# A two-layer encoder trunk in three-term fp32: last head pair filled further, operand orders at the feed-forward, unread retention states

## The chip, the cores and the metric

The kernel runs on one core of a Trainium2 chip. The metric is the device time of one execution in microseconds. A core has five engines that run their own instruction streams and meet at semaphores: TensorE (PE, matmuls into PSUM), VectorE (DVE), ScalarE (ACT), GpSimd (POOL) and SyncE (SP), which here issues all DMAs.

## What is computed

The reference, cut to its two layers. Layer 0 mixes tokens by bidirectional retention (six heads of 128), layer 1 by two-dimensional neighbourhood attention (twelve heads of 64, taken in six pairs); beside either stand four memory heads, and a SwiGLU feed-forward follows each. There are 1024 tokens of width 1024, a hidden width of 2816 and 256 memory tokens.

```
a = rms_norm(h, norm_g[i, 0])
y = retention_layer(a, ...) if i % 2 == 0 else na_layer(a, ...)     # concat heads and memory heads, @ w_out
h = h + rms_norm(y, norm_g[i, 1])
a = rms_norm(h, norm_g[i, 2])
gate, up = jnp.split(a @ ffn_w_in[i], 2, axis=-1)
h = h + rms_norm((jax.nn.silu(gate) * up) @ ffn_w_out[i], norm_g[i, 3])

# retention, one direction, chunks of 128 tokens
kv = jnp.einsum('bhncd,bhnce->nbhde', kc * k_dec, vc)
def step(state, kv_n):
    return state * chunk_dec + kv_n, state
_, prev = lax.scan(step, jnp.zeros((b, h, dk, dv)), kv)
out = out + jnp.einsum('bhncd,nbhde->bhnce', qc * q_dec, prev)
```

## The kernel before

**Products.** A large product is made of three matmuls (`three`, L2111 to L2116): each operand is split into a rounded part ("hi", written by ScalarE) and a remainder ("lo", written by VectorE for activations and by GpSimd for weights), and hi·hi, hi·lo and lo·hi are summed in PSUM. Weights come in units of 128 x 1024 through a ring of three slots: SP loads `stage` (`load_units`), ScalarE writes `whi` (`his`, L1057), GpSimd writes `wlo` (`los`, L827), and TensorE's last use frees the slot. All orders are written out by hand: each engine's program lists its operations, and a step waits for semaphore counts.

**Turnings.** `turn` number t transposes normed token tiles into `aT` or `AOP`: TensorE transposes, ScalarE evicts piece k as hi (L1104), VectorE makes lo (L1561). In `first_two` (turnings 2 and 6, ahead of each layer's mixer) the second half of the tokens is turned in two parts of four pieces (`turn_late`, L2158) among the first products.

**Retention.** Per head `chunk_states` multiplies keys by values for eight chunks and both directions (L2504), VectorE's `scan` runs the recurrence, and `chunk_outputs` adds three products per chunk (L2515 to L2517). The forward state of chunk 0 and the backward state of chunk 7 are zero.

**Feed-forward.** Its input and output products are a two-level scheme with seven products in place of eight. `AOP` holds seven operands: 1 and 2 are halves of the turned tokens, the others are sums ("7", "6", "5", "3") and the second tokens' late pieces ("4"), made on VectorE by `turn_second` (L1642 to L1659) and `lo_second` (L1666). Weight operands come from ScalarE (`operand_hi`, L1143) and GpSimd (`combine` L904, `operand_lo` L880). `hidden_sum` (L1681) adds a product's bank to what is there; product "4" waits for the sums "6" and "7". `turn_second` of TensorE (L2254, L2262) makes the late pieces; its last one waits for `gate_out(l, 5)` (L1163).

**Passage.** After the output product of a feed-forward, VectorE scales (L1589), adds the residual (`post_add`, L1598) and norms (`post_scale`, L1549), four token tiles each; ScalarE squares; GpSimd makes the factors (`post_factor` L854 to L856, `pre_factor` L839 and L840). In layer 0 the split of the unit U_NA + 1 stands behind all four squares on ScalarE and behind all four `post_factor` on GpSimd.

**Attention.** Six head pairs of 16 tiles; step T of 96 (+4) has scores, peak, exponential, scaling, transposes and values of neighbouring tiles on different engines. `filler(T)` puts one projection piece of the next pair (two matmul triples) into each step. For the last pair t = T - 80 counts its tiles; there 24 output rows (each one triple, first set, pieces k = 0 to 5) are spread over t = 1 to 19:

```
                if 0 < t < LAST:
                    for m in range(24 * (t - 1) // (LAST - 1), 24 * t // (LAST - 1)):
                        out_rows(1, 0, m // TT, range(m % TT, m % TT + 1), first_set_free(1))
```

The pieces of the concatenated heads are stored to HBM (`store_cat`) and fetched back (`cat_back`, L582) over the space of `aT` once all projections are made, then split by `cat_split` (ScalarE L1365, VectorE L1887) at t = 0, 2, 5, 8, 11, 14; pieces 6 and 7 follow behind the pair (`out_phase`), and piece 7 is written in place. `take_k` (L2065) copies a pair's keys, `take_q` its queries.

## Time and profile before

| | us |
|---|---|
| median of 3 runs | 2304.22 (2302.72 to 2304.95) |
| the profiled execution, its own time | 2304.31 |
| its span | 2302.5 |
| TensorE / weight load busy | 2245.8 (98%) / 1840.5 (80%) |
| VectorE / ScalarE / GpSimd busy | 1227.9 (53%) / 902.1 (39%) / 1074.2 (47%) |
| DMA | 279.11 MB, mean 121 GB/s |

The span runs from the first to the last instruction in the trace; the execution's own time has 1.8 us more. Busy time of TensorE is that of its matmuls; weight loads run beside them. An engine's idle time is put down to what released the instruction behind it; idle time of an engine that nobody waits for costs nothing. In the chain of work that ended last, TensorE has 87% of the span. A row of a timeline gives start and duration in us, then in brackets the idle time before it and what ended that. A row of a stretch (A:B) gives its length, the busy us and number of instructions of PE, PEld, DVE, ACT and POOL, TensorE's granted clock as a share of full speed, the busy share of the DMA engines, and GB/s.

### The profile page before, as it was taken

What the parts mean: (1) busy time and instruction counts of PE and PEld (TensorE: products, weight loads), DVE (VectorE), ACT (ScalarE), POOL (GpSimd) and SP (SyncE); (2) the same over time, 40 slices, a digit from 0 to 9 for tenths busy, and PEclk for the clock granted to TensorE, in tenths of its full rate; (3) what the DMA queues carried; (4) which work ended last, traced back from release to release, by engine and by line L of the source; (5) the groups of instructions that cost most, each with busy time, mean ns of one, the idle gap of its engine ahead of it and who ended that gap; (6) DMA issues with size and microseconds to landing.
All of it is one profiled execution on the core that took longest, in us unless ns stands there. A gap on an engine that the chain in (4) does not pass through costs nothing.

```text
span 2302.5 us, 32169 instructions
## 1 busy us (share of the span) xinstructions
PE 2245.8 (98%) x11948; PEld 1840.5 (80%) x11948; DVE 1227.9 (53%) x2065; ACT 902.1 (39%) x1793; POOL 1074.2 (47%) x777
## 2 busy tenths in 40 slices
PE   7999999999999999999999999999999999999998
PEld 6788888888788888888879867767878888888886
DVE  4644444546654444577753255555575444347767
ACT  5531111256223333344654345554642333334443
...
GB/s 215 46 83 46 47 46 46 129 167 108 115 132 138 110 96 110 214 213 95 107 178 102 138 91 103 68 129 120 193 81 131 159 103 108 103 103 327 97 96 156
DMA packets 138573, 279.11 MB, mean 121 GB/s; under 512 B 34531, under 2 KB 55602, under 8 KB 136370
## 3 DMA queue, kind: packets, MB, share of 16 engines
...
q14 instruction: 59, 0.48, 0.1%
HBM read 207.80 MB, written 69.23 MB: 120 GB/s over the span
## 4 chain that ended last, share of the span: by engine, by line
PE 87%; DVE 3%; POOL 2%; ACT 1%; issue 1%; DMA 1%; SPq 0%; DVEq 0%; POOLq 0%; ACTq 0%
PE PS L2114 26%; PE PS L2116 26%; PE PS L2115 26%; PE PS L2396 2%; PE PS L2583 2%; PE PS L2601 2%; PE PS L2504 1%; POOL wlo L827 1%; DVE SB L1851 1%; PE PS L2429 1%; PE PS L2492 1%; PE PS L2384 1%; POOL rstd L856 0%; PE PS L2517 0%; PE PS L2516 0%
## 5 line engine op out<-in xcount | busy, mean ns | idle before, releaser
L2114 PE MATMUL PS<-AOP,OPS 128*128 128x512 f32 x1216 | 474.3, 390 | 5.1 <-DVE AOP L1666 3.2
L2116 PE MATMUL PS<-AOP,OPS 128*128 128x512 f32 x1216 | 473.5, 389 | 0.0
L2115 PE MATMUL PS<-AOP,OPS 128*128 128x512 f32 x1216 | 473.4, 389 | 0.0
L827 POOL TENSOR_TENSOR wlo<-stage,whi 128x1024 fp32r<-128x1024 f32 (+1 forms) x88 | 207.8, 2366 | 407.5 <-ACT whi L1057 407.2
L880 POOL TENSOR_TENSOR OPS<-TW,OPS 128x512 fp32r<-128x512 f32 x176 | 260.8, 1497 | 77.3 <-ACT OPS L1143 77.3
L2114 PE MATMUL PS<-aT,whi 128*128 128x512 f32 (+1 forms) x672 | 273.7, 407 | 7.3 <-DVE bdK L1917 3.6
L2114 PEld LDWEIGHTS PS<-AOP,OPS 128*128 128x128 f32 x1216 | 228.3, 188 | 54.4 <-POOL OPS L880 4.0
L2116 PEld LDWEIGHTS PS<-AOP,OPS 128*128 128x128 f32 x1216 | 228.3, 188 | 47.5
L2115 PEld LDWEIGHTS PS<-AOP,OPS 128*128 128x128 f32 x1216 | 228.4, 188 | 47.1
L2116 PE MATMUL PS<-aT,wlo 128*128 128x512 f32 (+1 forms) x672 | 261.4, 389 | 0.0
L2115 PE MATMUL PS<-aT,whi 128*128 128x512 f32 (+1 forms) x672 | 260.5, 388 | 0.0
L2114 PE MATMUL PS<-OPS 128*128 128x512 f32 x616 | 240.3, 390 | 1.8 <-DVE Y L1756 1.8
L2116 PE MATMUL PS<-OPS 128*128 128x512 f32 x616 | 239.9, 389 | 0.0
L2115 PE MATMUL PS<-OPS 128*128 128x512 f32 x616 | 239.8, 389 | 0.0
L1143 ACT ACTIVATE OPS<-TW 128x512 fp32r<-128x512 f32 x176 | 106.5, 628 | 338.1 <-POOL TW L904 315.9
L880 POOL TENSOR_TENSOR OPS<-stage,OPS 128x512 fp32r<-128x512 f32 x128 | 173.4, 1358 | 53.1 <-ACT OPS L1143 48.8
L839 POOL TENSOR_SCALAR msq<-sumsq 128x1 f32<-128x1 f32 x42 | 23.5, 560 | 361.2 <-ACT junk L1076 359.5
L1681 DVE TENSOR_TENSOR up<-PS,u 128x512 f32<-128x512 f32 x88 | 60.8, 691 | 226.5 <-PE PS L2116 224.9
L1270 ACT ACTIVATE OPS<-SRAW 128x512 fp32r<-128x512 f32 x154 | 97.4, 632 | 206.8 <-PE PS L2116 206.8
L1713 DVE TENSOR_TENSOR OPS<-SRAW,OPS 128x512 fp32r<-128x512 f32 x154 | 106.3, 690 | 96.7 <-ACT OPS L1270 96.5
L2114 PEld LDWEIGHTS PS<-aT,whi 128*128 128x128 f32 x672 | 128.4, 191 | 34.8 <-issue 11.9
L2116 PEld LDWEIGHTS PS<-aT,wlo 128*128 128x128 f32 x672 | 128.0, 191 | 26.5
...
## 6 DMA issues: line engine op xcount, KB each, us to landing
stage<-in_w SPq DMA_DIRECT2D x100, 512.0 KB, 3.8
hidden_scratch<-HT SPq DMA_DIRECT2D x154, 256.0 KB, 2.2
SRAW<-hidden_scratch SPq DMA_DIRECT2D x154, 256.0 KB, 2.6
...
```

Source lines behind the costliest of these rows:

```text
L827: pool.tensor_tensor(wlo[:, slot, cols], stage[:, slot, cols], whi[:, slot, cols].bitcast(F32), ALU.subtract)\
L880: pool.tensor_tensor(place[:, 1, :], w1_operand(l, j, p), place[:, 0, :].bitcast(F32), ALU.subtract)\
L1143: act.activation(op_place(q)[:, 0, :], w1_operand(l, j, p), ACT.Copy).then_inc(o_hi, 1)
L1270: act.activation(OPS[:, s_op, 0, :], SRAW[:, s_slot(q), :], ACT.Copy).then_inc(g_hi, 1)
L1681: dve.tensor_tensor(dst, PS[:, in_bank(l, j, p), :], with_, ALU.add).then_inc(f_ed, 1)
L1713: dve.tensor_tensor(OPS[:, slot, 1, :], src, OPS[:, slot, 0, :].bitcast(F32), ALU.subtract).then_inc(g_lo, 1)
L2114: pe.matmul(dst, stat[0], mov[0], start=start, stop=False, skip_group_check=onto)
L2115: pe.matmul(dst, stat[0], mov[1], start=False, stop=False, skip_group_check=onto)
L2116: return pe.matmul(dst, stat[1], mov[0], start=False, stop=stop, skip_group_check=onto)
L2396: ins = pe.transpose(PS[0:keys, banks(r)[1], c * P:(c + 1) * P], SB[:, r % 3, c * width:c * width + keys], ident[:, :])
L2583: ins = pe.matmul(dst, qpair[half, g % 2, t, :], keys[:, :, (GW - KC) * w:(GW - KC) * w + KC], start=True, stop=True)
L2601: ins = pe.matmul(PS[half, 7, (t % 4) * GW:(t % 4 + 1) * GW], Vc[0:keys, g % 2, place, half], PT[0:keys, r % 3, col:col + GW], start=(c == ...
```

## The change

- Retention: the state products of chunk 0 (backward half) and chunk 7 (forward half), and the two output products with zero states, are left out.
- Turnings 2 and 6: the first part of `turn_late` now turns six pieces, the second two; the second waits for two remainders instead of four, and a new wait for six stands ahead of the second halves of the first unit.
- Feed-forward entry: VectorE splits piece 7 ahead of the first `post_add`; ScalarE does `gate_out(l, 5)` ahead of `raw_second`; VectorE does `lo_second` ahead of the sums "6" and "7".
- Passage in layer 0: the split of U_NA + 1 moves behind the second tile on ScalarE and GpSimd, and VectorE's scales lag two tiles behind its sums. An exponential of one column is issued ahead of the memory queries' copies.
- Attention: queries are copied in two halves, one step apart, with the weight split behind. In the last pair 28 output rows are spread over t = -1 to 18, pieces are split at t = -3, -1, 1, 3, 6, 9, 13, the first three are fetched while the last key unit is still projected (a new semaphore `k_last` counts its pieces), units U_OUT1 + 3, + 4, + 5 are split at t = 6, 12, 17 (before, + 3 at 11 and the others in `out_phase`), and three units more are loaded ahead of the next phase.

The diff, with renumbered waits left out and one line of context:

```diff
@@ -239,6 +239,7 @@
             sem(n) for n in ("s_mm", "s_add", "s_exp", "s_nrm", "s_tr", "pt_ev", "pv", "o_ev"))
+        k_last = sem("k_last")
         v_mm, v_ea, v_ed = sem("v_mm"), sem("v_ea"), sem("v_ed")
@@ -284,7 +285,11 @@
                 return 4 - D0[t // 4] + k % 4
-            return 4 + k % 4 if t in (2, 6) else k % 4 if t == 5 else k
+            if t in (2, 6):
+                return (4, 5, 6, 7, 1, 3, 4, 5)[k]
+            return k % 4 if t == 5 else k
+        LATE = 6
@@ -363,6 +368,8 @@
             return [item for at, item in enumerate(FIRST) if sum(cost[:at]) * steps // sum(cost) == t]
+        SPLIT_AT = (-3, -1, 1, 3, 6, 9, 13)
@@ -573,10 +580,10 @@
-            def cat_back(l, th, tiles):
+            def cat_back(l, th, tiles, free=None):
                 cols = slice(HALF * th, HALF * th + HALF)
-                sp.wait_ge(*USED[U_OUT[l] - 1])
+                sp.wait_ge(*(free or USED[U_OUT[l] - 1]))
                 for k in tiles:
@@ -793,18 +800,21 @@
             for hp in range(1, HP):
+                if hp == HP - 1:
+                    for k in range(3):
+                        cat_back(1, 0, [k], (k_last, 2 * k + 2))
                 load_units(U_NAH + 2 * hp + 7)
...
                 if hp == HP - 1:
-                    cat_back(1, 0, range(KD - 2))
+                    cat_back(1, 0, range(3, KD - 2))
                 store_cat(9 + hp)
...
             load_units(U_OUT1 + 5)
-            cat_back(1, 1, range(KD - 2))
-            for th in range(2):
-                cat_back(1, th, [KD - 2])
+            cat_back(1, 0, [KD - 2])
+            cat_back(1, 1, range(KD - 1))
+            load_units(U_OUT1 + 8)
             before_out(1)
@@ -959,19 +969,20 @@
                     post_factor(1 + 2 * l, 1, i)
+                    if l == 0 and i == 1:
+                        los(U_NA + 2)
                 if l == 0:
-                    los(U_NA + 2)
                     for i in range(TT):
...
-            pool.memset(minus_half[:, :], -0.5).then_inc(mh_rdy, 1)
-            pool.wait_ge(mh_rdy, 1)
+            pool.memset(minus_half[:, :], -0.5).then_inc(zer, 1)
+            pool.wait_ge(zer, 1)
             pre(0)
...
             pool.memset(kprod[:, :, :], 0.0).then_inc(zer, 1)
-            pool.wait_ge(zer, 2)
+            pool.wait_ge(zer, 3)
             los(2)
@@ -1092,7 +1103,7 @@
                         act.wait_ge(t_low, t // 4 + 1)
-                    if t in (2, 6) and k == 4:
+                    if t in (2, 6) and k == LATE:
                         act.wait_ge(t_done, turned(t))
@@ -1190,9 +1201,6 @@
                 U, s, t = U_OUT[l], 2 * l, 4 * l + 3
-                if l:
-                    his(U + 5)
-                    cat_split(l, range(KD - 2, KD - 1))
                 cat_split(l, range(KD - 1, KD))
@@ -1237,8 +1245,8 @@
                 operand_hi(l, 8)
+                gate_out(l, 5)
                 raw_second(l)
-                gate_out(l, 5)
                 hi_second(l)
@@ -1305,8 +1313,8 @@
                     square(Y1[:, i, 0:HALF], total(N_T + 8 * s + TT + i), g_ed, 24 * l + 21 + i, y_sq)
-                if l == 0:
-                    his(U_NA + 2)
+                    if l == 0 and i == 1:
+                        his(U_NA + 2)
                 post_out(s, 1)
@@ -1476,15 +1484,16 @@
             act.wait_ge(h_new, 16)
+            act.activation(gvar[:, 0:1], minus_half[:, 0:1], ACT.Exp)
             take(U_NA, MQ[:, 0, :])
...
-            def take_q(n, dst):
+            def take_q(n, dst, halves=range(2)):
                 act.wait_ge(*USED[n])
                 act.wait_ge(g_used, N_OUT_FF)
-                for th in range(2):
+                for th in halves:
                     for w in range(2):
@@ -1492,7 +1501,8 @@
                             ACT.Copy, scale=0.125)
-                ins.then_inc(ev_act, 1)
+                if 1 in halves:
+                    ins.then_inc(ev_act, 1)
@@ -1519,17 +1529,14 @@
                 t = T - (HP - 1) * ROWS
-                if t < 0 and T % KD == KD - 2:
-                    n = next_unit(T)
-                    if T % ROWS < KD:
-                        take_q(n, qpair[:, (T // ROWS + 1) % 2, :, :])
-                    his(n + RING + 1)
-                if t == 0:
-                    cat_split(1, range(1))
-                if t in (2, 5, 8, 11, 14):
-                    cat_split(1, [(t + 1) // 3])
-                    if t == 11:
-                        his(U_OUT1 + 4)
+                if t < 0 and T % ROWS in (KD - 2, KD - 1):
+                    take_q(next_unit(T), qpair[:, (T // ROWS + 1) % 2, :, :], (T % ROWS - KD + 2,))
+                if t < 0 and T % ROWS in (KD - 1, ROWS - 2):
+                    his(next_unit(T) + RING + 1)
+                if t in SPLIT_AT:
+                    cat_split(1, [SPLIT_AT.index(t)])
+                if t in (6, 12, 17):
+                    his(U_OUT1 + 4 + (6, 12, 17).index(t))
             out_phase(1)
@@ -1625,9 +1632,8 @@
                 post_half(s, 1, 1, 0)
-                turn(t, range(6, 7))
+                turn(t, range(6, 8))
                 post_add(s, 1, 0)
-                turn(t, range(7, 8))
                 for i in range(1, TT):
@@ -1766,9 +1772,9 @@
                 turn_second(l)
+                lo_second(l)
                 hidden_sum(l, 0, "6")
                 hidden_sum(l, 0, "7")
-                lo_second(l)
                 hidden_sum(l, 0, "5")
@@ -1813,7 +1819,11 @@
                         post_in_late(s, i - 1, 0)
-                post_out(s, 1)
+                for i in range(TT + 2):
+                    if i < TT:
+                        post_add(s, 1, i)
+                    if l == 0 and i >= 2:
+                        post_scale(s, 1, i - 2)
@@ -2100,10 +2110,8 @@
                     take_k(next_unit(T))
-                if t == 0:
-                    cat_split(1, range(1))
-                if t in (2, 5, 8, 11, 14):
-                    cat_split(1, [(t + 1) // 3])
+                if t in SPLIT_AT:
+                    cat_split(1, [SPLIT_AT.index(t)])
             out_phase(1)
@@ -2147,15 +2155,15 @@
                 if part:
-                    pe.wait_ge(a_lo, a_before(t) + 4)
+                    pe.wait_ge(a_lo, a_before(t) + KD - LATE)
                 elif t == 6:
...
                         pe.wait_ge(xs, tiles_before(t) + i + 1)
-                    for k in range(4):
-                        f = (4 * part + k) * P
-                        ins = pe.transpose(PS[:, 4 + k, i * P:(i + 1) * P], set_tiles(t)[:, i, f:f + P], ident[:, :])
+                    for k in range(LATE, KD) if part else range(LATE):
+                        ins = pe.transpose(PS[:, turn_bank(t, k), i * P:(i + 1) * P],
+                                           set_tiles(t)[:, i, k * P:(k + 1) * P], ident[:, :])
                     if part:
@@ -2178,6 +2186,8 @@
                     ins.then_inc(w_used, 1)
+                elif n == U_OUT1 - 1:
+                    ins.then_inc(k_last, 1)
@@ -2210,6 +2220,8 @@
                 turn_late(t, 1)
+                pe.wait_ge(a_lo, a_before(t) + LATE)
                 for k in range(KD):
@@ -2355,8 +2367,8 @@
                 t = 4 * l + 3
-                for k in range(6, KD):
-                    out_rows(l, 0, k, range(2 if l == 0 and k == 6 else 0, TT))
+                for k in range(6 + l, KD):
+                    out_rows(l, 0, k, range(2 if k == 6 else 0, TT))
                 for st, free in ((1, second), (2, third)):
@@ -2500,9 +2512,10 @@
                         pe.wait_ge(st_rdy, h)
-                    bank = (2, 3, 0, 1)[c // 2]
-                    ins = pe.matmul(PS[:, bank, 256 * (c % 2):256 * (c % 2) + 256], Ktok[:, c, :],
-                                    vfb[:, c, :, :].rearrange("p a c -> p (a c)"), start=True, stop=True)
+                    bank, at_c = (2, 3, 0, 1)[c // 2], 256 * (c % 2)
+                    d0, d1 = (0, 1) if c == 0 else (1, 2) if c == 7 else (0, 2)
+                    ins = pe.matmul(PS[:, bank, at_c + P * d0:at_c + P * d1], Ktok[:, c, :],
+                                    vfb[:, c, d0:d1, :].rearrange("p a c -> p (a c)"), start=True, stop=True)
                 ins.then_inc(kv_mm, 1)
@@ -2513,8 +2526,10 @@
                     pe.matmul(dst, ST[:, c, :], V[:, c, :], start=True, stop=False)
-                    pe.matmul(dst, qfb[:, 0, cc], states[:, c, 0, :], start=False, stop=False)
-                    ins = pe.matmul(dst, qfb[:, 1, cc], states[:, c, 1, :], start=False, stop=True)
+                    if c > 0:
+                        ins = pe.matmul(dst, qfb[:, 0, cc], states[:, c, 0, :], start=False, stop=(c == 7))
+                    if c < 7:
+                        ins = pe.matmul(dst, qfb[:, 1, cc], states[:, c, 1, :], start=False, stop=True)
                 ins.then_inc(out_mm, 1)
@@ -2608,8 +2623,8 @@
                     project(U_NAH + 2 + piece // KD, piece % KD)
-                if 0 < t < LAST:
-                    for m in range(24 * (t - 1) // (LAST - 1), 24 * t // (LAST - 1)):
+                if 0 <= t + 1 < LAST:
+                    for m in range(28 * (t + 1) // LAST, 28 * (t + 2) // LAST):
                         out_rows(1, 0, m // TT, range(m % TT, m % TT + 1), first_set_free(1))
...
             tiles = HP * ROWS
```

How it moves instructions, at three places. VectorE at the first feed-forward entry, from the last remainder of a sum on (L1659, now L1665); L1666 (now L1672) is `lo_second`, L1681 (now L1687) the sums. Before:

```order
L1659 TENSOR_TENSOR AOP<-S1R,AOP 128x2048
L1681 TENSOR_TENSOR u_96<-PS,s_95 128x512
L1681 TENSOR_TENSOR up_97<-PS,u_96 128x512
L1666 SCALAR_TENSOR_TENSOR AOP<-PS,gT,AOP 128x512 x4
L1681 TENSOR_TENSOR up_97<-PS,up_97 128x512
L1659 TENSOR_TENSOR AOP<-RAWA,AOP 128x2048
L1681 TENSOR_TENSOR sg_99<-PS,u_96 128x512
L1681 TENSOR_TENSOR up_100<-PS,u_96 128x512
```

and with the change:

```order
L1665 TENSOR_TENSOR AOP<-S1R,AOP 128x2048
L1672 SCALAR_TENSOR_TENSOR AOP<-PS,gT,AOP 128x512 x4
L1687 TENSOR_TENSOR u_96<-PS,s_95 128x512
L1687 TENSOR_TENSOR up_97<-PS,u_96 128x512
L1687 TENSOR_TENSOR up_97<-PS,up_97 128x512
L1665 TENSOR_TENSOR AOP<-RAWA,AOP 128x2048
L1687 TENSOR_TENSOR sg_99<-PS,u_96 128x512
L1687 TENSOR_TENSOR up_100<-PS,u_96 128x512
```

The four remainders of the late pieces moved ahead of two sums.

VectorE in the passage behind layer 0's feed-forward: L1589 (now L1596) scales by the gains, L1598 (now L1605) is `post_add`, L1549 (now L1556) `post_scale`, L1561 (now L1568) the turning. Before:

```order
L1589 TENSOR_TENSOR Y_104<-Y_104,gB 128x512 x2
L1598 SCALAR_TENSOR_TENSOR Hb<-Y_104,rstd,Hb 128x1024 x2
L1549 TENSOR_SCALAR Y_104<-Hb,rstd 128x1024
L1598 SCALAR_TENSOR_TENSOR Hb<-Y_104,rstd,Hb 128x1024
L1549 TENSOR_SCALAR Y_104<-Hb,rstd 128x1024
L1598 SCALAR_TENSOR_TENSOR Hb<-Y_104,rstd,Hb 128x1024
L1549 TENSOR_SCALAR Y_104<-Hb,rstd 128x1024 x2
L1561 SCALAR_TENSOR_TENSOR aT<-PS,gT,aT 128x512 x8
```

and with the change:

```order
L1596 TENSOR_TENSOR Y_104<-Y_104,gB 128x512 x2
L1605 SCALAR_TENSOR_TENSOR Hb<-Y_104,rstd,Hb 128x1024 x3
L1556 TENSOR_SCALAR Y_104<-Hb,rstd 128x1024
L1605 SCALAR_TENSOR_TENSOR Hb<-Y_104,rstd,Hb 128x1024
L1556 TENSOR_SCALAR Y_104<-Hb,rstd 128x1024 x3
L1568 SCALAR_TENSOR_TENSOR aT<-PS,gT,aT 128x512 x8
```

Three sums now stand ahead of the first scale.

TensorE from the scores of the tiles before the last pair on (t = -2 and -1): L2583 (now L2598) scores, L2601 (now L2616) values, L2396 (now L2408) transposes, `whi,catT` an output row. Before:

```order
L2583 MATMUL PS<-kTn,qpair 64x320 x4
L2601 MATMUL PS<-PT,Vc 64x64 x12
L2396 MATMUL PS<-ident,SB 120x128 x2
L2396 MATMUL PS<-ident,SB 80x128
L2396 MATMUL PS<-ident,SB 120x128 x2
L2396 MATMUL PS<-ident,SB 80x128
L2583 MATMUL PS<-kTn,qpair 64x320 x4
L2601 MATMUL PS<-PT,Vc 64x64 x12
L2396 MATMUL PS<-ident,SB 120x128 x2
L2396 MATMUL PS<-ident,SB 80x128
L2114 MATMUL PS<-whi,catT 128x512
L2115 MATMUL PS<-wlo,catT 128x512
```

and with the change:

```order
L2598 MATMUL PS<-kTn,qpair 64x320 x4
L2616 MATMUL PS<-PT,Vc 64x64 x12
L2408 MATMUL PS<-ident,SB 120x128 x2
L2408 MATMUL PS<-ident,SB 80x128
L2122 MATMUL PS<-whi,catT 128x512
L2123 MATMUL PS<-wlo,catT 128x512
L2124 MATMUL PS<-whi,catT 128x512
L2408 MATMUL PS<-ident,SB 120x128 x2
L2408 MATMUL PS<-ident,SB 80x128
L2122 MATMUL PS<-whi,catT 128x512
L2123 MATMUL PS<-wlo,catT 128x512
L2124 MATMUL PS<-whi,catT 128x512
```

An output row stands behind each tile's transposes, where none stood before.

## Rows read from the trace of the kernel before

**Rows 1.** The page, part 1: busy us, share of the span and instructions of each engine

```profile
PE 2245.8 (98%) x11948; PEld 1840.5 (80%) x11948; DVE 1227.9 (53%) x2065; ACT 902.1 (39%) x1793; POOL 1074.2 (47%) x777
```

**Rows 2.** Waits of TensorE: engine, line, releaser: us in total, times, longest us

```profile
PE PS L2114 <- DVE AOP L1666: 3.2, 2, 1.6
...
PE PS L2158 <- DVE Y L1549: 3.5, 3, 2.0
...
PE PS L2114 <- DVE AOP L1561: 1.5, 2, 0.8
...
PE PS L2262 <- ACT Hb L1163: 2.7, 2, 1.4
...
PE PS L2396 <- DVE SB L1851: 2.7, 6, 0.7
...
PE PS L2114 <- POOL wlo L827: 2.5, 2, 1.4
...
PE PS L2114 <- issue: 2.3, 1, 2.3
...
PE PS L2114 <- DVE catT L1887: 1.6, 1, 1.6
```

**Rows 3.** Timeline of TensorE, first head: start us, us, engine, line, operation, tiles, xcount

```profile
152.01 2.05 PE L2492 MATMUL PS<-qT,kT 128*128 128x128 f32 x16 [0.30 <-ACT Ktok L1440]
...
164.82 3.61 PE L2504 MATMUL PS<-vfb,Ktok 128*128 128x256 f32 x16
```

**Rows 4.** Timeline of TensorE and VectorE around the first layer's second turning

```profile
47.06 1.91 PE L2158 MATMUL PS<-ident,Y 128*128 128x128 f32 x16
...
49.73 2.73 DVE L1561 SCALAR_TENSOR_TENSOR aT<-PS,gT,aT 128x512 fp32r<-128x512 f32 x4 [7.13 <-ACT aT L1104]
...
54.23 0.48 PE L2114 MATMUL PS<-aT,whi 128*128 128x512 f32 x1
```

**Rows 5.** Timeline of ScalarE, VectorE and GpSimd, first feed-forward entry

```profile
551.36 2.42 ACT L1173 ACTIVATE RAWB<-PS,gT 128x512 f32<-128x512 f32 x4 [2.56 <-PE PS L2254]
...
570.90 3.38 DVE L1659 TENSOR_TENSOR AOP<-S1R,AOP 128x2048 fp32r<-128x2048 f32 x1
...
578.22 2.72 DVE L1666 SCALAR_TENSOR_TENSOR AOP<-PS,gT,AOP 128x512 fp32r<-128x512 f32 x4
...
581.60 3.35 POOL L904 TENSOR_TENSOR TW<-stage,TW 128x512 f32<-128x512 f32 x1
...
585.12 1.30 POOL L904 TENSOR_TENSOR TW<-stage,TW 128x512 f32<-128x512 f32 x1 [0.17 <-POOL TW L904]
```

**Rows 6.** Timeline of the passage, and the stretch from 1190 to 1194 us

```profile
1176.30 2.47 DVE L1598 SCALAR_TENSOR_TENSOR Hb<-Y,rstd,Hb 128x1024 f32<-128x1024 f32 x2
...
1177.96 3.04 POOL L827 TENSOR_TENSOR wlo<-stage,whi 128x1024 fp32r<-128x1024 f32 x1
...
1185.00 1.28 DVE L1598 SCALAR_TENSOR_TENSOR Hb<-Y,rstd,Hb 128x1024 f32<-128x1024 f32 x1
...
1188.46 0.75 DVE L1549 TENSOR_SCALAR Y<-Hb,rstd 128x1024 f32<-128x1024 f32 x1 [0.71 <-POOL rstd L840]
...
1189.28 1.10 PE L2158 MATMUL PS<-ident,Y 128*128 128x128 f32 x4 [0.81 <-DVE Y L1549]
...
1190.00:1194.00 4.00, 4.00 (x14) 3.20 (x13) 2.73 (x4) 2.42 (x4) 0.00 (x0) 0.66 0.00 0
```

**Rows 7.** The last head pair: its stretch, timeline of VectorE and GpSimd, one DMA issue

```profile
1528.40:1592.00 63.60, 54.55 (x491) 37.34 (x490) 34.73 (x96) 33.29 (x88) 10.62 (x5) 1.00 0.39 133
...
1528.33 1.28 DVE L2065 COPY kTn<-PS 128x512 f32<-128x512 f32 x2
...
1530.52 2.33 DVE L1851 TENSOR_SCALAR SB<-SB,rowinv 128x320 f32<-128x320 f32 x1
...
1530.31 2.36 POOL L827 TENSOR_TENSOR wlo<-stage,whi 128x1024 fp32r<-128x1024 f32 x1 [17.21 <-ACT whi L1057]
...
catf<-cat_scratch SPq DMA_DIRECT2D x28, 256.0 KB, 5.9
```

10 lines of the change are left out of this document (5 added, 5 removed).

## The prediction

> **What bounds the kernel now.** I read the page's busy shares first: TensorE is busy 2245.8 of 2302.5 us [rows 1]. Apart from the first 8 us and the last 11, time can go in two ways only: fewer TensorE instructions, or a wait of TensorE taken away. The view of waits shows them one by one [rows 2]: two of up to 1.6 us on the operands of the feed-forward entry (VectorE, L1666), two of 1.4 on a ScalarE eviction (L1163), two of up to 0.8 on the last operand (L1561), waits for turned tiles (L1549), weights (L827) and the last head pair's rows ("issue", L1887, L1851). All of these lie where the change works. In TensorE's timeline no wait of over 0.1 us lies between 600 and 1050 us or between 1190 and 1373, so time won ahead of those stretches should stay won.
>
> **Retention states.** Per head the state products are a run of 16 instructions of 256 columns in 3.61 us; sixteen of 128 columns take 2.05, some 0.12 each [rows 3]. The change halves four of the first kind (4 x 1.56 / 16 = 0.39) and drops four instructions of 128 columns in the output stage (0.48). Six heads: 6 x 0.87 = **5.2 us**. TensorE works without a break around them, so all of it counts. Bounds 5.0 and 5.3. Nobody waits for what goes.
>
> **Early turning of the first eight pieces.** Before, the first transposes start at 47.06, VectorE's remainders at 49.73, and the second halves of the projection at 54.23, 7.17 us after the start [rows 4]. Now eight more transposes come first (8 x 0.11 = 0.9), and a new wait asks for six remainders, not four, at 0.68 each (2.73 for four): 2.67 + 0.9 + 4.1 = 7.7. Behind the new wait stand only second-half products. Cost **+0.5** at the first use (bounds +0.2 and +0.8).
>
> **Feed-forward entry, twice.** The eighth piece is no longer split behind a sum that waits for GpSimd: 0.7 and 0.8 go. The eviction that TensorE's last transposes wait for stands ahead of the four of 2.42 us (551.36) instead of behind them: 1.4 goes [rows 2, 5]. The remainder at 578.22, for which TensorE waits 1.6, moves ahead of two sums; VectorE was free for it from 574.3 (570.90 + 3.38). That would make 3.6 per entry, but two things become late next. First, the same product also waits for the two sums, now behind the remainder: 574.3 less 0.4 (its chain starts that much sooner), plus 2.7, plus 2 x 0.7, is 578.0 in place of 580.9, so 2.9 to 3.0. Second, GpSimd: its subtraction at 581.60 took 3.35 us beside VectorE's large one against 1.30 for the next [rows 5]. With both chains shifted this collision falls on the weight operand that the next product needs, for 1 us or a little more. I take **1.9** per entry, **3.8** together; bounds 1.2 (GpSimd's whole lead gone) and 3.4 (no collision).
>
> **Passage from the first feed-forward to the second layer.** GpSimd's split of 3.04 us at 1177.96 stands between the factors of the sums and the factors of the next norm; TensorE waits 1.4 for it and VectorE holds its third sum behind the first scale [rows 2, 6]. Now that split sits two factors earlier and VectorE makes three sums first. ScalarE's copy delays the last two squares and so the first sum by about 0.6, from 1176.3 to 1176.9. Three sums of 1.24 [rows 6], a scale of 0.7 and the fourth sum end at 1182.5. From the last sum's end (1186.28) to its scale (1188.46) was 2.2, so the last scale starts at 1184.7, 3.8 sooner. TensorE follows 0.8 later, with six transposes (0.66) instead of four: 1186.2. Then it waits for six remainders, 1.0 to start and 4.1: 1191.3. Before, the transposes at 1189.28 were followed by 12 products in 4.1 us, because the granted clock was 0.66 there (full speed would be 2.7), and 16 transposes: 1195.8. Gain **4.5**. Bounds: 2.5, if VectorE's sums collide with the moved split for its whole 2.4 us; 5.0, if they don't collide at all.
>
> The exponential issued early moves a table load of ScalarE to where TensorE has products, and TensorE had no wait after it before either: nothing. If that cover were gone it would cost or give one load. The query copies in two parts and the moved weight splits of the earlier pairs: nothing, because no wait of TensorE is put down to them, and each weight is needed dozens of tiles later.
>
> **Last head pair.** TensorE is idle 63.60 - 54.55 = 9.05 us from 1528.4 to 1592 [rows 7]. Of these, 4.3 lie before the first output row (two tiles without filling, then 2.3 for the first piece), 2.1 in the middle, 2.6 after it (1.6 for a catT piece, 1.1 for a weight) [rows 2]. Now rows start at the tile before the pair. The first needs the keys' copy, which VectorE finishes at 1529.6 while TensorE is there at 1528.4 [rows 7]: 1.2 in place of 4.3. In the middle GpSimd splits three weights instead of one. A split at 1530.31 of 2.36 us made VectorE's scaling at 1530.52 take 2.33, not 0.4; TensorE waited 0.7 for it [rows 2, 7]. Two more such waits, less 0.9 since 28 rows fill better than 24: 2.6. At the end the weight is early, but the rows that stood behind the last head's values are used up: copy 0.5, ScalarE 0.6, VectorE 0.7, doubled where the last split runs, and hand-offs make 2.5. Idle 6.3, gain **2.7**. Bounds: a gain of 6 (no lock reaches TensorE), a loss of 0.9 (below).
> The Trainium skill says (SBUF — State Buffer, Who interferes with whom) that VectorE and GpSimd share one pair of ports as a lock: the first to issue keeps it for its whole instruction and the other stands still. The trace agrees: VectorE's scaling ended 0.2 us after GpSimd's split. By the full lock, 1.9 of each of three splits would reach TensorE and the pair would lose 0.9 rather than gain 2.7.
> On SP, two weight loads now stand behind the waits for the new pieces, behind TensorE's third-last tile before the pair; the first of them is split ten tiles (some 20 us) after that: nothing.
>
> **The sum.** -5.2 + 0.5 - 3.8 - 4.5 - 2.7 = -15.7 us. The profiled execution took 2304.31, 0.1 above the median 2304.22, so the sum holds for both: 2304.3 - 15.7 = **2288.6**.
>
> **The rivals.**
> *The lock reaches TensorE in full.* Each of three splits costs 2.33 - 0.39 = 1.9 us where the forecast has 0.7. For it: the scaling did stand still that long [rows 7]. Against it: only 0.7 got through, since a turned tile has some 2.4 us of other TensorE work between. The pair's 2.7 become a loss of 0.9: 2292.2.
> *Nothing is given back at the entries and in the passage.* If GpSimd stays ahead and does not collide, the entries give 6.8 and the passage 5.0: 2285.1. Against it: in the entries the two already take turns, at 3.4 us for an operation on both sides [rows 5], and TensorE would come 3 us sooner to what they make.
> *The moves only shift the waits.* Then the removed products alone remain, less the 0.5 of turning: 2304.3 - 4.7 = 2299.6. It needs entries, passage and pair to fail together.
> *Pieces arrive late.* ScalarE and VectorE take a piece in program order, so the next tiles' exponentials stand behind its transfer. A transfer took 5.9 us [rows 7]; three tiles ahead are 6.3. Before, TensorE stood 2.3 us for the first piece and 0.7 for the tile behind it [rows 2]. If all seven came so late, 7 x 3.0 = 21 us: 2309.6, slower than before. It turns to the slow side from 15.7 / 7 = 2.2 us per piece. Against it: the first three are asked for from 1511 on, five tiles ahead, and the others before the pair's fourth tile; only the seventh, stored late, is tight.
>
> **How the numbers follow.** About 0.2% (4.6 us) is what a measurement of this kernel can tell from no change. Forecast 0.60, full lock 0.17, nothing given back 0.13: all faster, 0.90. Moves only shift: 0.06, within 0.2%. Late pieces 0.04, of which I count all as slower. The sum of the kinder bounds is -5.3 + 0.2 - 6.8 - 5.0 - 6 = -22.9, of the harder ones -5.0 + 0.8 - 2.4 - 2.5 + 0.9 = -8.2. So the range is 2281.4 to 2296.1; I give 2281.5 to 2296.5.
>
> **What would show it.** State products of 128 columns at both ends of each head, and a head 0.87 us shorter from start to start. A wait of about 1.5 us of TensorE behind the second transposes in both turnings. No wait on L1163 and L1561 in the entries, a small one in place of the 1.6. The last scale of the passage near 1180 (1184.7 less what was won before). In the pair, a first wait of some 1.2 us behind the keys' copy, waits of 0.7 behind GpSimd's splits, one of 2.5 before the eighth piece, none for a weight. I am wrong if the pair's idle time is not between 3 and 10 us, if an entry still has 3 us of waits, or if a new wait opens on GpSimd between 600 and 660 us.

## The result and the profile after

The changed kernel takes 2287.91 us (median of 4 runs, 2287.14 to 2289.24), beside 2304.40 for the kernel before in the same comparison (2302.72 to 2304.95). The ratio is 0.993, 95% interval 0.9918 to 0.9942: 0.7% faster, a small change, but clear of the noise. 2288.6 was predicted, and 2281.5 to 2296.5 as the range. The sum was right; two of its terms were not, and their errors cancelled.

The profiled execution took 2287.36 us, its span 2285.6. The page's part 1, against [rows 1]:

```profile
PE 2238.6 (98%) x11924; PEld 1833.6 (80%) x11924; DVE 1226.3 (54%) x2065; ACT 901.6 (39%) x1794; POOL 1079.9 (47%) x777
```

TensorE is busy 7.2 us less; the other 9.7 us of the span are waits and gaps. To see where, I took the starts of the same instructions of TensorE in both traces ("shift" is after minus before):

| TensorE's instruction | before | after | shift | won or lost in the stretch (predicted) |
|---|---|---|---|---|
| first transposes of the first layer's tokens | 33.68 | 31.64 | -2.04 | start-up: -2.0 (0) |
| second turning: transposes | 47.06 | 45.04 | -2.02 | |
| its second halves | 54.23 | 52.69 | -1.54 | early turning: +0.5 (+0.5) |
| scores of retention head 1 | 152.01 | 150.52 | -1.49 | |
| last transpose of head 6's outputs | 456.10 | 449.65 | -6.45 | retention: -5.0 (-5.2) |
| 23rd feed-forward product | 600.77 | 592.06 | -8.71 | first entry: -2.3 (-1.9) |
| passage: second halves | 1195.79 | 1185.93 | -9.86 | passage: -1.1 (-4.5) |
| scores of the fifth pair | 1489.94 | 1480.47 | -9.47 | pairs: +0.4 (0) |
| output row 64 of the second layer | 1606.77 | 1592.14 | -14.63 | last pair: -5.2 (-2.7) |
| 23rd feed-forward product, second layer | 1722.30 | 1705.35 | -16.95 | second entry: -2.3 (-1.9) |
| last product | 2291.70 | 2274.74 | -16.96 | |

Most of the 2.0 of the start-up is not the change's. Twelve later profiles of the changed kernel and of kernels made from it, all with the same start-up, have that first instruction anywhere between 30.41 and 33.30. In the profile of the kernel before, TensorE was granted half its clock from 15.2 to 18.5 and from 28.8 to 32.2 us; in the changed kernel's it had full clock from 17 us on. e_gate_back (below), which has the changed start-up, fell to half clock in the same two places and has that instruction at 33.30, so at most 0.4 of the 2.0 is left for the change. Without the start-up the change moved 14.9 us where 15.7 were predicted.

**Retention and the first turning.** The group of the state products by form (least, median and longest ns), then TensorE's timeline, against [rows 3, 4]. Of a head's 16 state products four have 128 columns now (24 of 96 in the groups by line and form), the run takes 3.19 us instead of 3.61, and TensorE goes from one head's scores to the next in 56.57 us instead of 57.40. In the turning the new wait for six remainders is there, behind eight second transposes:

```profile
L2517 PE MATMUL PS<-vfb,Ktok x96: 270/379/382, 163.3 to 431.0; 128*128 128x256 f32 x72, 128*128 128x128 f32 x24
```

```profile
163.32 3.19 PE L2517 MATMUL PS<-vfb,Ktok 128*128 128x128 f32 x16
```

```profile
45.04 2.79 PE L2165 MATMUL PS<-ident,Y 128*128 128x128 f32 x24
...
50.40 1.04 PE L2165 MATMUL PS<-ident,Y 128*128 128x128 f32 x8
52.69 0.50 PE L2122 MATMUL PS<-aT,whi 128*128 128x512 f32 x1 [1.25 <-DVE aT L1568]
```

**Entries.** TensorE's waits from 530 to 600 us. The 1.4 on the eviction, the 1.6 on the remainder and the 0.7 for the eighth piece [rows 2] are gone; what is left is GpSimd's:

```profile
PE PS L2122 <- POOL OPS L890: 1.2, 2, 0.9
```

In the timeline of GpSimd and TensorE the product (1,"6") starts when GpSimd's weight operand for it ends (579.71 plus half of 2.52; the row groups two operations):

```profile
579.71 2.52 POOL L890 TENSOR_TENSOR OPS<-TW,OPS 128x512 fp32r<-128x512 f32 x2
```

```profile
568.76 0.50 PE L2122 MATMUL PS<-AOP,OPS 128*128 128x512 f32 x1 [0.28 <-POOL OPS L890]
...
581.04 0.50 PE L2122 MATMUL PS<-AOP,OPS 128*128 128x512 f32 x1 [0.88 <-POOL OPS L890]
```

**Passage.** The timelines of VectorE and GpSimd, against [rows 6]:

```profile
1166.52 3.10 DVE L1596 TENSOR_TENSOR Y<-Y,gB 128x512 f32<-128x512 f32 x2 [0.33 <-ACT junk L1087]
1169.54 3.66 DVE L1605 SCALAR_TENSOR_TENSOR Hb<-Y,rstd,Hb 128x1024 f32<-128x1024 f32 x3
1173.93 0.75 DVE L1556 TENSOR_SCALAR Y<-Hb,rstd 128x1024 f32<-128x1024 f32 x1 [0.72 <-POOL rstd L850]
1174.60 1.28 DVE L1605 SCALAR_TENSOR_TENSOR Hb<-Y,rstd,Hb 128x1024 f32<-128x1024 f32 x1
1176.31 0.75 DVE L1556 TENSOR_SCALAR Y<-Hb,rstd 128x1024 f32<-128x1024 f32 x1 [0.44 <-POOL rstd L850]
1177.78 0.75 DVE L1556 TENSOR_SCALAR Y<-Hb,rstd 128x1024 f32<-128x1024 f32 x1 [0.71 <-POOL rstd L850]
1179.25 0.75 DVE L1556 TENSOR_SCALAR Y<-Hb,rstd 128x1024 f32<-128x1024 f32 x1 [0.71 <-POOL rstd L850]
```

```profile
1165.11 0.36 POOL L864 TENSOR_TENSOR msq<-sumsq,halfsq 128x1 f32<-128x1 f32 x1
1165.55 0.55 POOL L866 TENSOR_TENSOR rstd<-msq,minus_half 128x1 f32<-128x1 f32 x1
1166.07 2.40 POOL L837 TENSOR_TENSOR wlo<-stage,whi 128x1024 fp32r<-128x1024 f32 x1
...
1170.00 0.86 POOL L864 TENSOR_TENSOR msq<-sumsq,halfsq 128x1 f32<-128x1 f32 x1
1170.94 1.48 POOL L866 TENSOR_TENSOR rstd<-msq,minus_half 128x1 f32<-128x1 f32 x1
...
1173.98 0.75 POOL L849 TENSOR_SCALAR msq<-sumsq 128x1 f32<-128x1 f32 x1
1174.81 1.47 POOL L850 TENSOR_TENSOR rstd<-msq,minus_half 128x1 f32<-128x1 f32 x1
```

Every scale waits for GpSimd. GpSimd has no pause of over 0.1 us from 1164.59 to 1179.21. Of its two operations on one column for a factor, the first takes 0.2 us alone, but 0.75 beside a scale (1173.98 to 1174.73 beside VectorE's 1173.93 to 1174.68); the second takes 0.55 alone, but 1.47 beside a sum. The last scale starts at 1179.25; shifted like the stretch before, it would have started at 1179.74 without the change (1188.46 - 8.72). So only 0.5 of the 3.8 us came. From the last scale to the second halves it is 6.68 us, where it was 7.33 (1188.46 to 1195.79).

**Last pair.** TensorE's waits from 1514 to 1570 us, against [rows 2, 7]: 5.25 us in five waits, where it had been idle for 9.05. In the trace the 1.4 in the second line are 0.40 at 1544.62 and 1.02 at 1558.50:

```profile
PE PS L2122 <- DVE catT L1897: 2.3, 1, 2.3
PE PS L2408 <- ACT PT L1347: 1.4, 2, 1.0
PE PS L2122 <- DVE kTn L2075: 1.2, 1, 1.2
PE PS L2408 <- DVE SB L1861: 0.3, 1, 0.3
```

### The profile page after: what moved, and what is told of

It is laid out like the page before. It is cut to its first block, busy times and chain, and to the rows that moved or that the text cites. A ratio compares the mean times of both kernels' runs of the same rounds, so it can differ in the third digit from the quotient of the medians.

```text
span 2285.6 us, 32133 instructions
## 1 busy us (share of the span) xinstructions
PE 2238.6 (98%) x11924; PEld 1833.6 (80%) x11924; DVE 1226.3 (54%) x2065; ACT 901.6 (39%) x1794; POOL 1079.9 (47%) x777
## 4 chain that ended last, share of the span: by engine, by line
PE 86%; POOL 4%; DVE 2%; ACT 2%; issue 1%; DMA 0%; POOLq 0%; DVEq 0%; ACTq 0%
PE PS L2122 26%; PE PS L2124 25%; PE PS L2123 25%; PE PS L2408 2%; POOL OPS L890 2%; PE PS L2616 2%; PE PS L2598 1%; PE PS L2517 1%; POOL TW L914 1%; PE PS L2441 1%; PE PS L2504 1%; PE PS L2396 1%; PE PS L2528 0%; DVE SB L1861 0%; PE PS L2530 0%
## 5 line engine op out<-in xcount | busy, mean ns | idle before, releaser
L890 POOL TENSOR_TENSOR OPS<-TW,OPS 128x512 fp32r<-128x512 f32 x176 | 266.2, 1526 | 77.3 <-ACT OPS L1154 77.3
L890 POOL TENSOR_TENSOR OPS<-stage,OPS 128x512 fp32r<-128x512 f32 x128 | 179.2, 1403 | 48.8 <-ACT OPS L1154 44.8
L1687 DVE TENSOR_TENSOR up<-PS,u 128x512 f32<-128x512 f32 x88 | 60.8, 691 | 225.2 <-PE PS L2124 223.6
```

Of the source, the lines that this page charges most:

```text
L890: pool.tensor_tensor(place[:, 1, :], w1_operand(l, j, p), place[:, 0, :].bitcast(F32), ALU.subtract)\
L1687: dve.tensor_tensor(dst, PS[:, in_bank(l, j, p), :], with_, ALU.add).then_inc(f_ed, 1)
```

## The experiments

Each kernel is the changed one with one edit or, where said, several. Since start-ups differ by up to 2.9 us between profiled executions, a stretch is read from its own first to its own last instruction of TensorE, and single times are given less the shift of the instruction ahead of the stretch; most waits repeat to 0.05 us. What does not repeat is the stretch in which TensorE is granted half its clock, and a wait of 0.2 to 0.6 us for a normed tile in a feed-forward entry. The medians (4 or 5 runs each) are less sharp: the 95% intervals of their ratios are 5 to 8 us wide, so an effect of 1 or 2 us is read from the traces, one profile of each kernel, and not from the medians.

### The passage: place of the split, order of the sums

```
p_split_back (GpSimd; on ScalarE the same behind the four squares)
-                    if l == 0 and i == 1:
-                        los(U_NA + 2)
+                if l == 0:
+                    los(U_NA + 2)
p_order_back (VectorE)
-                for i in range(TT + 2):
...
+                post_out(s, 1)
p_sums_first = p_split_back, and on VectorE
+                for i in range(TT):
+                    post_add(s, 1, i)
+                for i in range(TT if l == 0 else 0):
+                    post_scale(s, 1, i)
```

> The changed kernel with one thing undone: the weight split of the passage stands again behind the fourth factor of the sums (on ScalarE behind the four squares), VectorE's new order of sums and scales is kept. Theory A (GpSimd's row of one-column factor operations sets the last scale, and the moved split of 2.4 us pushes the third and fourth of them back by 2): the first sum starts near 1168.2 instead of 1169.54, the last scale near 1177.5 instead of 1179.25, and the kernel is 1 to 2 us faster than the changed one, even with a short wait of TensorE for the weight. Theory B (the place of the split is right, VectorE's collisions cost the rest wherever it stands): the last scale is 1 to 3 us later than 1179.25.

> The changed kernel with VectorE's old order of sums and scales in the passage (sum, sum, scale, sum, scale, sum, scale, scale), split where the change has it. Theory A: the third sum stands behind the first scale, which GpSimd's factor sets at 1173.9; from there sum, square, factors and scale follow twice, and the last scale starts near 1181.6 instead of 1179.25: 2.3 us slower than the changed kernel, slower in this place than before. Theory B (the order of the sums gives nothing once the split stands earlier): the last scale stays within 0.5 us of 1179.25.

> The changed kernel with the split back behind the fourth factor and VectorE making all four sums before the first scale. Theory A: sums from 1168.2 to 1173.3, squares done at 1174.4, the last factor at 1175.9 and the last scale near 1176.0, 3.2 us sooner than 1179.25; some 2 to 3 us faster than the changed kernel, since TensorE's transposes then follow each other. Theory B (the collisions of GpSimd's split with the sums cost what the order gives): last scale at 1178 or later, less than 1 us gained.

| | median us | first sum | last scale | TensorE's second halves, against the changed kernel |
|---|---|---|---|---|
| changed | 2287.91 | 1169.54 | 1179.25 | 0 |
| p_split_back | 2289.31 | 1167.59 | 1179.42 | +0.03 |
| p_order_back | 2288.90 | 1169.54 | 1179.90 | +0.99 |
| p_sums_first | 2288.35 | 1167.59 | 1179.42 | +0.03 |

Both theories fell for the split. With the split back the first sum does come 1.9 us sooner, but the split then takes 3.04 us beside the sums, and stretches the third of them to 3.39. The time goes from one place of GpSimd's row to another, and the end stays. The same for four sums ahead of the scales: they are made by 1174.6, and the scales follow 1.47 us apart all the same; theory B's numbers came there (the last scale at 1178 or later, nothing gained). VectorE's old order makes the last scale 0.65 us later, between the two theories' 2.3 and 0.5. Of its 0.99 the other 0.34 is the clock: in p_order_back it was half from 1180.9 to 1184.2, among the products behind the last scale, and in the changed kernel from 1177.0 to 1180.3, among transposes. So the new order is worth 0.65 us, a quarter of what I expected. From the timeline of p_sums_first, GpSimd and VectorE:

```profile
1173.54 1.47 POOL L850 TENSOR_TENSOR rstd<-msq,minus_half 128x1 f32<-128x1 f32 x1
1175.10 0.75 POOL L849 TENSOR_SCALAR msq<-sumsq 128x1 f32<-128x1 f32 x1
1175.94 0.55 POOL L850 TENSOR_TENSOR rstd<-msq,minus_half 128x1 f32<-128x1 f32 x1
```

```profile
1175.05 0.75 DVE L1555 TENSOR_SCALAR Y<-Hb,rstd 128x1024 f32<-128x1024 f32 x1 [0.45 <-POOL rstd L850]
1176.52 0.75 DVE L1555 TENSOR_SCALAR Y<-Hb,rstd 128x1024 f32<-128x1024 f32 x1 [0.72 <-POOL rstd L850]
```

The next factor's first operation starts with the scale and ends with it; its second, 0.55 us, and the hand-offs follow, and only then the next scale can start. That gave a new theory: the number of GpSimd's operations sets the end.

```
p_pairs = p_sums_first, and on GpSimd
-                        pre_factor(1, 1, i)          (four times: two operations on one column)
+                    for i in (0, 2):
+                        pool.wait_ge(pre_sq, xi + 2)
+                        link(pool.tensor_scalar(msq[:, xi:xi + 2], sumsq[:, xi:xi + 2], ...))
+                        pool.tensor_tensor(rstd[:, xi:xi + 2], msq[:, xi:xi + 2], minus_half[:, 0:2], ALU.pow)
```

> The kernel of the run p_sums_first (split behind the fourth factor, four sums before the scales) with GpSimd's eight operations on one column for the last four norm factors done as four on two columns each. Theory A (the row of GpSimd operations, each stretched beside VectorE, sets the last scale; each factor came 1.47 us after the one before): the last scale, 1179.46 in p_sums_first with its start-up taken as equal, comes 1.5 to 2 us sooner, near 1177.6, and TensorE's second halves begin as much sooner. Theory B (ScalarE's squares or VectorE's own row set it): within 0.4 us of 1179.46, since the last square ends at about 1175.8 in both.

Median 2287.43 us. VectorE's timeline:

```profile
1168.45 6.97 DVE L1608 SCALAR_TENSOR_TENSOR Hb<-Y,rstd,Hb 128x1024 f32<-128x1024 f32 x4
1176.03 1.42 DVE L1559 TENSOR_SCALAR Y<-Hb,rstd 128x1024 f32<-128x1024 f32 x2 [0.60 <-POOL rstd L978]
1178.03 1.42 DVE L1559 TENSOR_SCALAR Y<-Hb,rstd 128x1024 f32<-128x1024 f32 x2 [0.59 <-POOL rstd L978]
```

The last scale starts at 1178.70, less 0.86 of shift 1177.84, which is 1.6 sooner than in p_sums_first; TensorE's second halves come 1.6 us sooner as well (1.55 against the changed kernel). Theory A holds: it is the row of GpSimd operations. In p_pairs it is no longer the only bound: GpSimd stands 0.70 us before the second pair's first operation (1176.70), and ScalarE's last square ends at 1176.61.

### The entry: which edit pays

```
e_lo_back (VectorE, both layers)          e_gate_back (ScalarE, both layers)
-                lo_second(l)             -                gate_out(l, 5)
                 hidden_sum(l, 0, "6")                     raw_second(l)
                 hidden_sum(l, 0, "7")    +                gate_out(l, 5)
+                lo_second(l)                              hi_second(l)
e_mixed: first layer both of these; second layer only
-                turn(t, range(6, 8))
+                turn(t, range(6, 7))
                 post_add(s, 1, 0)
+                turn(t, range(7, 8))
```

> The changed kernel with VectorE's remainder of the entry (four operations, 2.7 us) back behind its two sums, in both layers; ScalarE's order and the eighth piece stay as changed. Theory A (the edits of an entry only pay together, since TensorE reaches the same product sooner): TensorE waits 3 us or a little more for that remainder where before it waited 1.6, the two new waits for GpSimd go, and each entry is 1.9 us longer than in the changed kernel, 3.8 us together. Theory B (each edit pays for itself): the old wait of 1.6 comes back in place of the 1.2 for GpSimd, 0.4 to 0.7 us per entry, 1.4 at most together.

> The changed kernel with only ScalarE's order in the entry undone: the eviction that TensorE's last four transposes wait for stands again behind the four copies, in both layers. Undoing VectorE's remainder alone moved an entry by 0.1 us. Theory A (GpSimd's row of weight operands ends each entry at nearly the same time, so no single order is worth its wait): the eviction's wait of 1.4 us comes back, the waits of 0.28 and 0.88 us for GpSimd shrink, and each entry is 0.2 to 0.8 us longer. Theory B (this eviction is the one edit of the entry that pays): each entry is 1.4 us or more longer, with GpSimd's waits unchanged.

> The changed kernel with the entry's edits undone in other groups, one per layer. First layer: ScalarE's eviction and VectorE's remainder both back where they stood (each alone changed this entry by 0.1 us). Second layer: only VectorE's split of the eighth piece back behind the sum. Theory A (an entry ends with GpSimd's weight operand for the product (1,6); each order alone is worth nothing, because the next one and that operand allow the same end, and only when both are back does TensorE come later than GpSimd): the first entry is 1.3 to 2.0 us longer than in the changed kernel, with waits of 1.4 for the eviction and 1.5 or more for the remainder; the second 0 to 0.4 longer, though the wait of 0.7 for the eighth piece is back. Theory B (the effects add): the first entry 0.2 us longer, and the eighth piece accounts for the rest of the 2.3: the second 1.9 or more.

Medians 2287.53, 2288.41 and 2290.78 us. The length of an entry against the changed kernel's, by the 23rd product, and TensorE's waits in the first entry (in the nine other profiles, whose entries are as in the changed kernel, the first entry comes out between -0.3 and +0.3 us and the second between -0.2 and +0.5):

| | first entry | second entry | waits, first entry |
|---|---|---|---|
| e_lo_back | -0.2 | -0.2 | 1.0 remainder, 0.3 GpSimd |
| e_gate_back | +0.1 | -0.4 | 1.4 eviction, 0.6 a normed tile, 0.1 GpSimd |
| e_mixed | +2.1 | +0.7 | 1.6 remainder, 1.4 eviction, 0.7, 0.2 |

The three longest waits of e_mixed from 535 to 600 us:

```profile
PE PS L2130 <- DVE AOP L1677: 1.6, 1, 1.6
PE PS L2282 <- ACT Hb L1174: 1.4, 1, 1.4
PE PS L2274 <- DVE Y L1559: 0.7, 1, 0.7
```

Undoing VectorE's remainder costs nothing: both theories of e_lo_back fell. Undoing ScalarE's eviction costs nothing either, though its wait of 1.4 is back; the 0.28 and 0.88 us for GpSimd become 0 and 0.12, as theory A of e_gate_back had it, without even the 0.2 us that it expected. Both undone cost 2.1 of the entry's 2.3 us, just above theory A's 2.0, where theory B had 0.2. As long as either is done, TensorE meets GpSimd's operand for (1,"6") with a margin of 0.05 to 0.1 us; only with both undone does it come 1.7 later than GpSimd (in the kernel before, the operand ended at 587.67 and the product began at 589.35). The operand itself ends 131.1 to 131.6 us behind the last transpose of head 6's outputs in all five profiles, those of the kernel before and of the changed one included: none of the orders moves it. The second entry of e_mixed, with only the eighth piece back, is 0.7 us longer (0.4 at most was expected), and its wait of 0.7 is back; since an unedited second entry came out 0.5 longer once, the size is uncertain. In the first entry next to nothing is left for the eighth piece (2.3 - 2.1, within the scatter). So the effects do not add: the orders lead to one bound, and how much the eighth piece is worth by itself stays open.

### The last pair: more rows, or fewer splits

```
f_rows24:  -  for m in range(28 * (t + 1) // LAST, 28 * (t + 2) // LAST):
           +  for m in range(24 * (t + 1) // LAST, 24 * (t + 2) // LAST):
g_splits_late (ScalarE):
-                if t in (6, 12, 17):
-                    his(U_OUT1 + 4 + (6, 12, 17).index(t))
+                if t == 6:
+                    his(U_OUT1 + 4)
 (the other two in out_phase, the first ahead of the eighth piece)
```

> The changed kernel with 24 instead of 28 output rows between the tiles of the last head pair (the seventh piece's four rows come behind the pair). Theory A (more filling covers waits of the pair): the pair up to the last values is 2.7 us shorter by the rows that went (4 rows of three products at 0.227) less 0.5 to 1 us of waits that lose their cover; behind it the four rows hide the wait of 2.3 us for the eighth piece. From the pair's first scores to output row 64 the two are within 1 us of each other, and the number 28 is not what brought the gain. Theory B (28 rows are worth it): row 64 comes 1.5 us later or more than with 28.

> The changed kernel with the two later weight splits of the last pair (at its tiles 12 and 17) taken behind the pair; the one at tile 6 stays. Theory A (GpSimd's split holds VectorE up, and so TensorE): the wait of 1.02 us in the pair's second half goes to under 0.2 us, the 0.34 and 0.40 behind the first split stay, and the wait for the eighth piece grows by up to 1 us, as ScalarE's copy of a weight now stands ahead of it. Theory B (the wait of 1.02 comes from the pieces' own splits on ScalarE and VectorE): it stays within 0.2 us of 1.02.

Medians 2286.99 and 2288.72 us. The waits of f_rows24, and of g_splits_late, from 1514 to 1570 us:

```profile
PE PS L2408 <- ACT PT L1347: 2.0, 3, 1.0
PE PS L2122 <- DVE kTn L2075: 1.2, 1, 1.2
PE PS L2122 <- DVE catT L1897: 0.4, 1, 0.4
PE PS L2408 <- DVE SB L1861: 0.3, 1, 0.3
```

```profile
PE PS L2124 <- DVE catT L1899: 2.3, 1, 2.3
PE PS L2124 <- DVE kTn L2077: 1.2, 1, 1.2
PE PS L2410 <- ACT PT L1349: 0.4, 1, 0.4
PE PS L2410 <- DVE SB L1863: 0.3, 1, 0.3
```

With 24 rows the wait for the eighth piece goes from 2.33 to 0.43, and the pair has one wait of 0.6 and some small ones more: row 64 comes 0.8 us sooner than with 28. Theory A holds, and further than I had it: the gain of the last pair does not come from the number 28. By the waits, the largest part is that rows begin before the pair (4.3 us idle ahead of the first row before, one wait of 1.16 now); no run undid that alone. With two splits behind the pair the wait of 1.02 is gone, the two behind the first split stay, and nothing grows at the end: 1.0 us by row 64, theory A again. Its place in the changed kernel's timeline (VectorE's remainder of a piece took 1.54 us beside the split, and the next tile's peak stood behind it; such remainders take 0.68 alone):

```profile
1553.90 2.38 POOL L837 TENSOR_TENSOR wlo<-stage,whi 128x1024 fp32r<-128x1024 f32 x1 [11.18 <-ACT whi L1068]
```

```profile
1555.29 1.54 DVE L1897 TENSOR_TENSOR catT<-catf,catT 128x512 fp32r<-128x512 f32 x1 [1.77 <-ACT catT L1373]
```

### Turning, retention, query copies

Three edits undone in one kernel, since they lie far apart: `LATE = 4`, the products of unread states made again, `take_q` whole at its old place.

> The changed kernel with three edits undone that lie in different stretches. Turning: 4 instead of 6 pieces turned in the first group, in both layers. Expected: from the first transposes of the first turning to the second halves 0.5 us less; in the second layer's passage 0.3 to 0.5 less as well, as two remainders fewer are waited for (rival: the six early pieces pay in the passage, where it comes out 0.3 or more longer). Retention: the state products and the output products of unread states are computed again (their result is not used): 0.83 us per head more, 5.0 in all. Query copies of the pairs whole at their old place, weight splits too: five pairs 0.3 to 0.4 us less if the halves cost something on TensorE, 0 if they don't. The kernel as a whole is 3.5 to 4.5 us slower than the changed one.

Median 2293.57 us. The first turning is 0.47 shorter. Head for head 0.83 or 0.84 comes back, 5.02 in all. From the passage to the fifth pair it wins 0.38 us; this undoes the halved copies and the moved weight splits together, so it does not say which of the two costs it. These three are as expected. The passage went the rival's way, 1.85 us longer, and so the kernel is 5.0 to 5.7 us slower than the changed one by the medians, not 3.5 to 4.5. The reason is in the windows of u_three at 1184.2 to 1189.5 us (columns: stretch, length, busy of PE, PEld, DVE, ACT and POOL, granted clock, DMA share, GB/s) and in the same products of the changed kernel:

```profile
1184.20:1189.50 5.30, 5.30 (x15) 4.05 (x14) 2.73 (x4) 2.42 (x4) 0.00 (x0) 0.50 0.00 0
```

```profile
1180.80:1183.70 2.90, 2.90 (x16) 2.35 (x15) 1.87 (x3) 2.59 (x5) 0.00 (x0) 1.00 0.00 0
```

Twelve products ran at half clock (1.2 GHz) in 5.3 us instead of 2.8. In the changed kernel the clock fell too (0.70 granted from 1175 to 1180), but there TensorE was making short transposes between waits; it was back before the products. Less those 2.4 us, four pieces would be 0.6 us shorter here as well.

The other profiles show what six pieces do. From the start of the last scale to the second halves:

| | pieces turned early | clock at half, us | last scale to second halves |
|---|---|---|---|
| e_lo_back, p_split_back, p_sums_first | six | not at all | 6.54 |
| changed | six | 1177.0 to 1180.3 | 6.68 |
| p_order_back | six | 1180.9 to 1184.2 | 7.02 |
| g_splits_late | six | 1177.8 to 1184.5 | 7.21 |
| before | four | 1189.4 to 1192.7 | 7.33 |
| u_three | four | 1182.8 to 1189.5 | 8.55 |

With six pieces TensorE waits 1.2 us for six remainders; when products run slower this wait shrinks (0.44 in g_splits_late, none in p_order_back) and takes up part of the loss. With four pieces there is no such wait. The two rows with four pieces come to an estimated 6.1 at full clock (7.33 less 1.25, 8.55 less 2.4, what the twelve products lost). So the 1.85 us are the clock's: by this estimate six pieces cost 0.4 at full clock and save where it falls on the products. No profile has four pieces in the passage at full clock.

### What paid, together

`best` joins p_pairs, f_rows24, g_splits_late, whole query copies, and four early pieces in the first turning with six in the second. It ran beside the unedited changed kernel.

> The changed kernel once more, unedited, beside the next run on the same chip: 2287 to 2289 us. Its profile should repeat all waits to 0.05 us; what may differ is the start-up (up to 2.4 us so far) and the granted clock behind the wait of 2.3 us for the eighth piece (output rows 28 to 32 took 2.9 us in the first profile and in three runs, 4.0 to 4.5 in the others).

> The changed kernel with what single runs showed to pay: in the passage the split back behind the fourth factor, four sums first, norm factors in pairs (-1.5 us); four early pieces in the first turning, six in the second (-0.5); query copies whole (-0.4); 24 rows between the last pair's tiles (-0.8); two weight splits of the last pair behind it (-1.0). If these add up, since they lie in different stretches, it is 4.2 us faster than the changed kernel, near 2283.7 us, perhaps 1 us more because the clock no longer falls behind a wait of 2.3 us. Rival: the two edits of the last pair do not add, because with 24 rows the weight that is split behind the pair is needed at once: then 2.5 us faster.

| | median us (runs) | against before | 95% interval |
|---|---|---|---|
| changed, again | 2288.58 (2286.97 to 2289.21) | 0.9928 | 0.9914 to 0.9941 |
| best | 2283.45 (2282.56 to 2283.77) | 0.9905 | 0.9891 to 0.9918 |

5.1 us lie between the medians, and no run of one falls among those of the other. 4.2 was expected, and the rival's 2.5 fell. By the traces the turning gives 0.5, the passage 1.6, the pairs 0.4 and the last pair 2.6, where 0.8 and 1.0 alone would make 1.8: with both edits the eighth piece is no longer waited for at all. The waits of best from 1514 to 1570 us, 2.5 in all:

```profile
PE PS L2129 <- DVE kTn L2082: 1.2, 1, 1.2
PE PS L2415 <- ACT PT L1354: 1.0, 2, 0.6
PE PS L2415 <- DVE SB L1868: 0.3, 1, 0.3
```

## Why the prediction was right, and where it was wrong

**The sum: right, and so close by luck.** 2288.6 against 2287.91. The passage brought 3.4 us less than its term and the pairs lost 0.4 that I had at nothing; the last pair brought 2.5 and the two entries 0.8 more than theirs. In the traces 14.9 us came of 15.7, and the medians lie 16.5 apart, which their intervals do not tell from either.

**Retention: right.** 5.0 measured by the change and 5.02 by its undoing, against 5.2; the bounds were 5.0 to 5.3.

**Early turning: right.** +0.47 against +0.5, with a wait of 1.25 behind the second transposes.

**Entries: near in size (2.3 each, against 1.9), half right in mechanism.** The step "the same product also waits for the two sums, now behind the remainder: 578.0 in place of 580.9" failed: that product had no wait at all (568.76 and 581.04 are the only ones), since VectorE was not late. (The upper bound of 3.4, "no collision", did not fit this step's own 2.9 to 3.0 either.) What I had as the second bound was the only one: the collision on the weight operand "for 1 us or a little more" is the 0.88 at (1,"6"), with 0.28 for (0,"5") four products earlier. I took the three edits as three gains less a bound. The runs show one bound that any of several orders reaches: VectorE's new order could have been left out.

**Passage: wrong, 1.1 against 4.5, below its bound of 2.5.** Two steps failed. First, "the split delays the first sum by 0.6, to 1176.9": in before's times it started at 1178.26 (1169.54 + 8.72), because VectorE's two multiplications took 3.10 us beside the moved split, not 1.4. Second, "from the last sum's end to its scale was 2.2, so the last scale starts at 1184.7". I carried this distance over as if only ScalarE's square and one factor lay in it. In fact it was GpSimd's queue: from the fourth sum's end (1175.87) to the last scale (1179.25) it was now 3.4. I counted GpSimd's split and not its sixteen operations on one column, each of which is stretched whenever VectorE works beside it. Neither the other place of the split nor four sums ahead (p_split_back, p_sums_first) got past that row; p_pairs, with four operations fewer, did. The third step held: from the last scale to the second halves the term had 6.6 us (1184.7 to 1191.3), and it is 6.68. But that gain, 0.65 of the 1.1, hangs on where the clock fell: before, on the twelve products (1.25 lost); now, on transposes (0.14, against the profiles where it did not fall). With full clock on both sides the passage would have won an estimated 0.1 (0.5 at the last scale, less 0.4 for six pieces).
The Trainium skill's rule (SBUF — State Buffer, Who interferes with whom), that the first of VectorE and GpSimd to issue keeps the shared ports for its whole instruction, fits these rows better than I used it: GpSimd's 128x1 operation beside a scale ended 0.05 us after the scale, not at 0.2 of its own.

**Last pair: right in sign, wrong in size, 5.2 against 2.7.** By term: the start 1.16 (1.2 predicted), the middle 1.76 (2.6), the end 2.33 (2.5), no wait for a weight: 5.25 against 6.3. Among the waits the middle was the mis-sized one; of three splits the first cost 0.34 + 0.40, the second 1.02 and the third nothing that shows. With the first idle time of 9.05 this explains 3.8 us. The larger miss is a term that I did not have at all: the remaining 1.4 lie in TensorE's own pace between scores and row 64. Between two products of rows it took 242 ns on average without waits before (174 times) and 239 now (172), which makes 1.0 us, with six interruptions of over 0.1 us in place of eleven. That fewer interruptions are the cause is likely, not shown; I did not separate this further.
The full lock was a rival at 0.17. The trace has it in the instructions (1.92 for a scaling of 0.41 at 1541.01, 1.54 for a remainder of 0.68). Of it 0.74 behind the first split and 1.02 behind the second reached TensorE, not 1.9 each.

**Priced at nothing: the query copies in halves, with the weight splits moved behind them,** cost 0.4 us up to the fifth pair; no single wait over 0.1 us shows it, and the cause inside the pairs stays open. No cost of the table load shows, and TensorE never waited for a fetched piece's transfer.

Of the signs I had named, the 128-column products, the wait of 1.5 (1.25), the two waits that vanish in the entries, the first and the last wait of the pair all came; no new wait opened between 600 and 660 us. The last scale "near 1180" came at 1179.25, and this sign was badly chosen: 1184.7 less the 8.7 won before is 1176.0, so 1179.25 stood for a failure, not for a success.
